# A hybrid diffusion layer on one core: the middle stage reordered

## The reference

```python
h = rmsnorm(x, norm1_g) * (1 + sc1) + sh1
z = h @ w_in                                  # 1280 columns
u_ssm, u_pool, u_conv = z[..., :512], z[..., 512:768], z[..., 768:]
# A) two-way diagonal complex scan (32 groups of 16 channels, 64 states), then
y = gelu(y); y_ssm = y * sigmoid(y @ w_glu + b_glu)
# B) pooling: mean over centred windows 2/4/8/16 minus the token, 64x64 linear per group, scale
# C) v = a * sigmoid(g); depthwise convolution of width 31; LayerNorm over 256 channels; silu
x = x + g1 * (concat(y_ssm, y_pool, y_conv) @ w_out)
h2 = rmsnorm(x, norm2_g) * (1 + sc2) + sh2
x = x + g2 * ((silu(h2 @ w1) * (h2 @ w3)) @ w2)
```

## Time and profile before

| | us |
|---|---|
| runs (median; lowest, highest) | 1330.0; 1328.51, 1331.0 |
| the profiled execution: span from the first to the last instruction | 1323.8 |
| PE busy (share of the span) | 1220.8 (92%) |
| DVE busy | 850.8 (64%) |
| ACT busy | 511.0 (39%) |
| POOL busy | 516.0 (39%) |

### The profile page before, as it was taken

How to read it: one execution, slowest core, us unless ns; L and a number is a source line. 1 busy time by engine, 2 the same in 40 slices (tenths; PEclk the granted TensorE clock), 3 DMA queues, 4 the chain that set the end, 5 groups by cost and what they waited for, 6 DMA issues and landing times.

```text
span 1323.8 us, 21436 instructions
## 1 busy us (share of the span) xinstructions
PE 1220.8 (92%) x7574; PEld 1080.5 (82%) x7574; DVE 850.8 (64%) x1338; ACT 511.0 (39%) x911; POOL 516.0 (39%) x360
## 2 busy tenths in 40 slices
PE   6786978995599999899999999999999999999996
PEld 4486877895545788799999999999889999999995
DVE  5538539959973427677666667766865555555558
ACT  2652531117235646633333333333532333334223
POOL 0595104376233101654444455444443233333340
PEclk9897988898799999999999999999999999999998
DMA  8815054389791331866665766666768777777771
GB/s 308 339 64 157 28 163 150 105 95 211 204 400 64 128 112 64 270 225 221 206 217 187 246 222 227 217 207 220 260 193 276 246 256 256 260 254 263 244 275 75
DMA packets 189570, 268.52 MB, mean 203 GB/s; under 512 B 14031, under 2 KB 108537, under 8 KB 186825
## 3 DMA queue, kind: packets, MB, share of 16 engines
q1 hardware_dynamic: 188144, 263.07, 60.6%
q0 software_dynamic: 1280, 4.72, 0.9%
q10 hardware_dynamic: 88, 0.02, 0.0%
HBM read 186.49 MB, written 81.26 MB: 202 GB/s over the span
## 4 chain that ended last, share of the span: by engine, by line
PE 76%; DMA 5%; issue 4%; POOL 4%; ACT 4%; DVE 3%; SPq 3%; DVEq 0%; ACTq 0%; POOLq 0%
PE banks L862 22%; PE banks L864 22%; PE banks L863 22%; PE banks L1131 3%; DMA ad<-in_ada_w 1%; PE banks L898 1%; PE banks L947 1%; SPq L436 1%; ACT nts L1660 1%; PE banks L1013 1%; POOL psum_w L751 1%; POOL sst L791 1%; DMA z_dram<-zp 1%; POOL pu L757 1%; PE banks L1136 1%
## 5 line engine op out<-in xcount | busy, mean ns | idle before, releaser
L814 POOL TENSOR_TENSOR raw13r<-raw13s,w13h 128x512 fp32r<-128x512 f32 x110 | 155.1, 1418 | 467.1 <-ACT w13h L1612 421.9
L863 PE MATMUL banks<-ntr,w13h 128*128 128x256 f32 (+1 forms) x1144 | 336.1, 294 | 0.0
L862 PE MATMUL banks<-ntr,w13h 128*128 128x256 f32 (+1 forms) x968 | 282.5, 292 | 4.4 <-ACT xs L1622 2.3
L863 PEld LDWEIGHTS banks<-ntr,w13h 128*128 128x128 f32 x1144 | 215.5, 188 | 0.9
L862 PEld LDWEIGHTS banks<-ntr,w13h 128*128 128x128 f32 x968 | 182.5, 189 | 6.5 <-ACT xs L1622 2.6
L862 PE MATMUL banks<-f2h,f_hi 128*128 128x512 f32 x396 | 156.6, 395 | 0.4 <-DVE acc L2317 0.4
L864 PE MATMUL banks<-f2h,f_lo 128*128 128x512 f32 x396 | 156.2, 395 | 0.0
L863 PE MATMUL banks<-f2l,f_hi 128*128 128x512 f32 x396 | 156.2, 394 | 0.0
L864 PE MATMUL banks<-ntr,raw13r 128*128 128x256 f32 (+1 forms) x528 | 153.5, 291 | 0.0
L2183 DVE TENSOR_TENSOR acc<-acc,banks 128x512 f32<-128x512 f32 x170 | 112.7, 684 | 38.9 <-PE banks L864 30.8
L818 POOL TENSOR_TENSOR f2l<-f2s,f2h 128x1024 fp32r<-128x1024 f32 x44 | 106.1, 2432 | 34.1 <-ACT f2h L1616 34.1
(11 more groups left out here) (323 smaller groups left out, 2536.4 us busy)
## 6 DMA issues: line engine op xcount, KB each, us to landing
raw13s<-in_ffn_w SPq DMA_DIRECT2D x66, 512.0 KB, 4.5
parts<-w13h SPq DMA_DIRECT2D x110, 256.0 KB, 2.4
w13h<-parts SPq DMA_DIRECT2D x110, 256.0 KB, 2.7
f2s<-in_ffn_w SPq DMA_DIRECT2D x44, 512.0 KB, 4.2
ad<-in_ada_w SPq DMA_DIRECT2D x20, 1024.0 KB, 9.8
parts<-wsumr SPq DMA_DIRECT2D x66, 256.0 KB, 2.6
wsumr<-parts SPq DMA_DIRECT2D x55, 256.0 KB, 4.9
parts<-raw13r SPq DMA_DIRECT2D x44, 256.0 KB, 2.9
```

The lines of the kernel that those rows point to most:

```text
L814: nc.gpsimd.tensor_tensor(w13_low(x, f), w13_low(x, f, F32), w13h[x][:, :, :].bitcast(F32), ALU.subtract).then_inc(sem("w13_lo"), 1)
L862: nc.tensor.matmul(out, hi_w, hi_x, start=start, stop=False)
L863: nc.tensor.matmul(out, hi_w, lo_x, start=False, stop=False)
```

## The change

It does seven things.

1. `sst` is split into four quarter buffers. Quarter 0 lies in the buffer of the pooling windows (`psum_w`), and is copied by POOL alone, all 8 copies, right after the pooling, ahead of the second gate of the convolution input and without waiting for the input projection's end. Of quarters 1 to 3 POOL copies the rows r = 0 and ACT the rows r = 1, in the order of the quarters. `yb` moves to where the copy of quarter 0 was.
2. The first gate of the convolution input goes ahead of the second half of the pooling's second part (`gate_conv(0)` after `w_low(9)`).
3. `u9` has four buffers. Re-reads 2 and 3 are issued after the `wc` reads of quarters 1 and 2, no longer in the transposes' loop.
4. Of quarter 3's eight writes of y four are issued by ACT.
5. PE runs GLU tile 2, the rest of adaLN group 2, and GLU tile 3 directly; the first channel means come behind them, then three of the blocks' first products, and only then the second channel means. ACT's squares and roots move behind `y_high(3)`, its SiLUs to the end of the stage.
6. `OUT` takes y parts 2 and 3 before the convolution's 6 and 7.
7. The low parts of y parts 0 to 3 go from DVE to POOL, one after each `wo_low`.

The diff, with the changed lines and some of those around them:

```diff
--- before.py
+++ after.py
@@ -200,14 +200,14 @@
-    u9 = [at(f"u9{i}", [P, 8, UC], O_UZ + 9216 + 4608 * i) for i in range(2)]
+    u9 = [at(f"u9{i}", [P, 8, UC], a) for i, a in enumerate((O_UZ + 9216, O_UZ + 13824, O_WS + 9216, O_WS + 13824))]
...
-    sst = at("sst", [P, 2, Q, UC], O_NT + 36864)
+    sst = [at(f"sst{e}", [P, 2, 2, 4, UC], O_WB + 9408 if e == 0 else O_NT + 36864 + 9216 * e) for e in range(4)]
...
-    yb = [at(f"yb{i}", [P, 8, UC], O_WB + 9408 + 4608 * i) for i in range(2)]
+    yb = [at(f"yb{i}", [P, 8, UC], O_NT + 36864 + 4608 * i) for i in range(2)]
@@ -217,7 +217,7 @@
-    OUT = (4, 5, 0, 1, 6, 7, 2, 3)
+    OUT = (4, 5, 0, 1, 2, 3, 6, 7)
@@ -347,6 +347,11 @@
     def low_ready(i):
...
+
+    def row_copy(e, r, d, par):
+
+        return (view(sst[e], (2 * par + d) * 4 * UC, [[UC, 4], [BL, NBL], [1, BL]], NS * r, NS),
+                view(st, r * Q * SLOTS + NPAIR * d + 4 * e, [[1, 4], [Q, NBL], [SLOT, BL]], NS * par, NS))
@@ -458,7 +463,7 @@
         def u_again(j):
...
-                sp.dma_start(u9[j % 2][16 * s:16 * s + 16, :, :],
+                sp.dma_start(u9[j][16 * s:16 * s + 16, :, :],
@@ -478,6 +483,8 @@
+            if e in (1, 2):
+                u_again(e + 1)
         def out_weights(n):
@@ -487,16 +494,15 @@
-            if j + 2 < 4:
-                sp.wait_ge(sem("y_done"), 2 * (j + 1))
-                u_again(j + 2)
-            for t in range(CH):
+            for t in range(CH if j < 3 else CH // 2):
...
-                sp.wait_ge(sem("st_copied_act"), 16)
-                sp.wait_ge(sem("st_copied_pool"), 16)
-            sp.wait_ge(sem("y_out"), 16 * 8 * (j + 1))
+                sp.wait_ge(sem("st_copied_act"), 12)
+                sp.wait_ge(sem("st_copied_pool"), 20)
+            if j == 3:
+                sp.wait_ge(sem("y_out_act"), 64)
+            sp.wait_ge(sem("y_out"), 16 * 8 * (j + 1) if j < 3 else 448)
@@ -527,7 +533,7 @@
-        sp.wait_ge(sem("y_low_dve"), 4)
+        sp.wait_ge(sem("y_part_pool"), 6)
...
         def w13_in(pr, f, tile, first=False):
@@ -734,6 +740,12 @@
+        def gate_conv(j):
+            pool.wait_ge(sem("z_evac"), NB * (8 + 2 * j))
+            for a0, b0, n in ((PAD, 0, LAT), (PAD + LAT + PAD, LAT, CTX)):
+                nc.gpsimd.tensor_tensor(vp[:, j, a0:a0 + n], vp[:, j, a0:a0 + n], sig[:, j, b0:b0 + n], ALU.mult).then_inc(sem("gated"), 1)
+            pool.wait_ge(sem("gated"), 2 * (j + 1))
+
@@ -757,12 +769,17 @@
+                    if j == 1:
+                        gate_conv(0)
...
-        for j in range(2):
-            pool.wait_ge(sem("z_evac"), NB * (8 + 2 * j))
-            for a0, b0, n in ((PAD, 0, LAT), (PAD + LAT + PAD, LAT, CTX)):
-                nc.gpsimd.tensor_tensor(vp[:, j, a0:a0 + n], vp[:, j, a0:a0 + n], sig[:, j, b0:b0 + n], ALU.mult).then_inc(sem("gated"), 1)
+        pool.wait_ge(sem("scan_done"), 1)
+        for r in range(2):
+            for d in range(2):
+                for par in range(2):
+                    nc.gpsimd.tensor_copy(*row_copy(0, r, d, par)).then_inc(sem("st_copied_pool"), 1)
+        pool.wait_ge(sem("st_copied_pool"), 8)
+        gate_conv(1)
         def wo_low(n):
@@ -776,20 +793,16 @@
-                pool.wait_ge(sem("y_low_dve"), m - 1)
+                pool.wait_ge(sem("y_part_pool"), m + 1)
...
-        pool.wait_ge(sem("gated"), 4)
...
-        pool.wait_ge(sem("scan_done"), 1)
-        for e in (0, 2):
-            for r in range(2):
-                for d in range(2):
-                    q0 = NPAIR * d + 4 * e
-                    for par in range(2):
-                        nc.gpsimd.tensor_copy(view(sst, (par * Q + q0) * UC, [[UC, 4], [BL, NBL], [1, BL]], NS * r, NS),
-                                              view(st, r * Q * SLOTS + q0, [[1, 4], [Q, NBL], [SLOT, BL]], NS * par, NS)).then_inc(sem("st_copied_pool"), 1)
+        for e in range(1, 4):
+            for d in range(2):
+                for par in range(2):
+                    nc.gpsimd.tensor_copy(*row_copy(e, 0, d, par)).then_inc(sem("st_copied_pool"), 1)
+        pool.wait_ge(sem("st_copied_pool"), 20)
@@ -797,6 +810,7 @@
+            y_low(m, ym[m % 2][:, :], m + 3)
@@ -1100,16 +1114,18 @@
-                pe.wait_ge(sem("st_copied_act" if j % 2 else "st_copied_pool"), 8 * (j // 2 + 1))
+                pe.wait_ge(sem("st_copied_pool"), 8 + 4 * j)
+                if j:
+                    pe.wait_ge(sem("st_copied_act"), 4 * j)
...
-                    mm(out, toep[:, 2 * gp + par, :], u9[j % 2][:, (2 * gp + par) % 8, :], start=True, stop=False)
-                    mm(out, wc[:, par, gp, HD:HD + P], sst[:, par, gp, :], start=False, stop=False)
-                    last = mm(out, wc[:, par, NPAIR + gp, 0:P], sst[:, par, NPAIR + gp, ::-1], start=False, stop=True)
+                    mm(out, toep[:, 2 * gp + par, :], u9[j][:, (2 * gp + par) % 8, :], start=True, stop=False)
+                    mm(out, wc[:, par, gp, HD:HD + P], sst[j][:, par, 0, gp % 4, :], start=False, stop=False)
+                    last = mm(out, wc[:, par, NPAIR + gp, 0:P], sst[j][:, par, 1, gp % 4, ::-1], start=False, stop=True)
@@ -1143,18 +1159,14 @@
+        glu_tile(2)
+        ada_tiles(2, 3, KT, B[4])
+        ada_bias_add(2, B[4])
+        glu_tile(3)
...
-        glu_tile(2)
-        for b in range(NB):
-            pe.wait_ge(sem("dev_squared"), 2 * (b + 1))
-            channel_mean([lnw[:, 0, :], lnw[:, 1, :]], b)
-        ada_tiles(2, 3, 6, B[4])
-        glu_tile(3)
-        ada_tiles(2, 6, KT, B[4])
-        ada_bias_add(2, B[4])
-        ready = {4: ("y_part_pool", 1), 5: ("y_part_pool", 2), 0: ("y_low_dve", 1), 1: ("y_low_dve", 2), 2: ("y_low_dve", 3), 3: ("y_low_dve", 4),
+        ready = {4: ("y_part_pool", 1), 5: ("y_part_pool", 2), 0: ("y_part_pool", 3), 1: ("y_part_pool", 4), 2: ("y_part_pool", 5), 3: ("y_part_pool", 6),
...
         def out_part(c, n0, n1, wait=False):
@@ -1175,14 +1187,17 @@
+        for b in range(NB):
+            pe.wait_ge(sem("dev_squared"), 2 * (b + 1))
+            channel_mean([lnw[:, 0, :], lnw[:, 1, :]], b)
...
+        for c in range(4):
+            out_part(c, 4, 6, c == 0)
...
-        for c in range(4):
-            out_part(c, 4, 6, c == 0)
@@ -1481,12 +1496,9 @@
         def state_copy(e):
-            for r in range(2):
-                for d in range(2):
-                    q0 = NPAIR * d + 4 * e
-                    for par in range(2):
-                        A_(view(sst, (par * Q + q0) * UC, [[UC, 4], [BL, NBL], [1, BL]], NS * r, NS),
-                           view(st, r * Q * SLOTS + q0, [[1, 4], [Q, NBL], [SLOT, BL]], NS * par, NS), ACT.Copy).then_inc(sem("st_copied_act"), 1)
+            for d in range(2):
+                for par in range(2):
+                    A_(*row_copy(e, 1, d, par), ACT.Copy).then_inc(sem("st_copied_act"), 1)
         def y_out(c):
@@ -1509,13 +1521,18 @@
+        state_copy(2)
+        y_out(2)
+        y_out(3)
...
-        for c in range(2, 6):
+        for c in range(4, 8):
...
+        act.wait_ge(sem("y_evac"), 16)
+        for t in range(CH // 2, CH):
+            act.dma_start(dview(y_dram, 3 * P * CH * UC + t * UC, [[CH * UC, 16], [16 * CH * UC, 8], [1, UC]]),
+                          yb[1][16 * t:16 * t + 16, :, :]).then_inc(sem("y_out_act"), 16)
...
-        y_out(6)
...
-        y_out(7)
@@ -1547,7 +1564,6 @@
-        act.wait_ge(sem("y_out"), 512)
@@ -1558,29 +1574,30 @@
+        glu_gate(2)
+        wo_high(4)
+        act.wait_ge(sem("scan_done"), 1)
+        mod_row_out(2, B[4])
+        act.wait_ge(sem("ada_tile"), 2 * KT + 4)
+        act.wait_ge(sem("glu_made"), 3)
+        y_high(2, ym[0][:, :])
+        glu_gate(3)
+        wo_high(5)
+        act.wait_ge(sem("glu_made"), 4)
+        y_high(3, ym[1][:, :])
...
-        glu_gate(2)
-        wo_high(4)
...
-        glu_gate(3)
-        act.wait_ge(sem("scan_done"), 1)
-        mod_row_out(2, B[4])
-        wo_high(5)
-        act.wait_ge(sem("ada_tile"), 2 * KT + 4)
-        conv_silu(0)
...
-        conv_silu(1)
-        for m in (2, 3):
-            act.wait_ge(sem("glu_made"), m + 1)
-            y_high(m, ym[m % 2][:, :])
...
+        conv_silu(0)
+        conv_silu(1)
@@ -2024,10 +2041,6 @@
-        def y_low(m):
-            dve.wait_ge(sem("y_part_act"), m + 3)
-            TT(y_lo[m][:, :], ym[m % 2][:, :], y_hi[m][:, :].bitcast(F32), ALU.subtract).then_inc(sem("y_low_dve"), 1)
-
@@ -2049,8 +2062,6 @@
-        y_low(0)
-        y_low(1)
@@ -2061,8 +2072,6 @@
-        y_low(2)
-        y_low(3)
...

```

## The result

The changed kernel takes 1336.71 us as the median of 10 runs (1332.80 to 1343.44), the kernel before 1328.03 (10 runs, 1322.40 to 1332.47): ratio 1.0068, 95% interval 1.0046 to 1.0090, so slower, by about 9 us. The profiled run of the changed kernel took 1342.24 us with a span of 1340.4.

The account below looks back on a forecast made before the run. The prediction took the chain of waits, mostly TensorE's products, to bound the kernel; -3.5 (transposes) + 2.4 (adaLN stall) + 5.4 (tail) + 2.0 (clock) = +6.3 on 1330.0 gave 1336.3 us, 8-in-10 range 1328 to 1342.

Parts of the forecast that it names:

- part (b): SyncE's y transposes, write, landing and read-back four times: GLU starts at 359.6 instead of 363.06, -3.5 us.
- the tail: Output products from the second channel means on: TensorE waits for y parts 6 and 7, +5.4 us (4.4 to 6.5).
- Part (a): Convolution gate and state-row copies on POOL: taps about 7.3 us earlier, first y product near 308, worth 0.
- take 8.3: Transposes, first to second read-back: 8.3 us instead of 12.6, as re-read 3 leaves this step.
- second to third stays 6.2: Transposes: the step from second to third read-back keeps its 6.2 us.
- 4.4: Transposes, third to fourth read-back: 4.4 us instead of 7.0, with GELUs done earlier and half the writes on ACT.
- The rule of ring order: DMA queue ahead of the y write: descriptors go in ring order, so re-read 3 delays the first read-back 3.5 us.
- rival 2: First y write passes the queue: first read-back at 327, GLU at 349.3, sum -4.0, 1326.0 us; chance 0.13.
- The adaLN stall: Last adaLN group after GLU tile 2: TensorE waits for tile 7's load, +2.4 us (1.0 to 4).
- table 1.28: ACT, after the scaling and before the SiLU pairs: a table load of 1.28 us on the way to y6.
- The clock: TensorE's granted clock falls after the tail's two gaps, +2.0 us (0 to 3); for the adaLN gap 0.
- Rival 3: Both gaps pull the clock down long and the last ada load meets other traffic: +12.4, 1342.4 us; chance 0.12.

Follow-up runs that it names:

- experiment 1: Changed kernel with the new order of TensorE's work, OUT and low parts undone; copies, buffers, re-reads and write split stay: 1328.05 us, ratio 1.0001 to before.
- experiment 7: Changed kernel with re-read 3 issued behind the first quarter's y writes instead of ahead of them: 1331.96 us (1 run).
- experiment 8: Changed kernel with GLU and output weights issued while SyncE waits for y writes to land, and adaLN biases put to the end: 1328.98 us (1 run).
- experiment 3: Changed kernel with adaLN tile 3 of group 2 made ahead of GLU tile 2 instead of behind it: 1333.3 us (1 run).
- experiment 9: kernel 4 with the first channel means between adaLN tiles 6 and 7 of group 2: 1325.23 us (1 run).
- experiment 2: Kernel before with only the new order of GLU, adaLN, means and y parts, and low parts on POOL: 1335.38 us, ratio 1.0058.
- kernel 4: Changed kernel with first means and squares ahead of GLU tile 3, second means right behind it, roots ahead of y_high(3): 1335.76 us (1 run).
- kernel 12: kernel 10 with re-read 3 behind the first y writes, ahead of the state-copy wait, and output weights behind the second and third quarters' writes: 1320.94 us, ratio 0.9928.
- kernel 5: Kernel before, with POOL waiting for VectorE's subtraction w_lo(1) before the third piece of wc: 1326.69 us, ratio 0.9997.
- experiment 6: Kernel before, with VectorE holding w_lo(1) until POOL has begun its wc products, so that both run together: 1329.82 us (1 run).
- kernel 10: Kernel of experiment 9 with the loads of experiment 8 and the wait of kernel 5: 1321.34 us, ratio 0.9943.

## Why the prediction was right, and where its sum was not

Forecast 1336.3, measured 1336.71. From R to c4 the sum gave +6.3, and the traces give 150.6 for 144.2, +6.4. But that exactness is luck: two errors cancel, part (b) 2.7 too good and the tail 2.5 too bad. That the times agree within 0.4 is luck too: the base of 1330.0 was 2.0 above the median of ten runs, and the change 2.4 more than forecast.

- **Part (a), 0.** Right in result: experiment 1 moves G by 0.4. The copies and taps moved as worked out (the taps end 77.0 after R for 84.5, so 7.5 earlier, forecast 7.3); TensorE reads them only at 420.00, so no one was waiting. The first y product, 8.1 after R, was expected 8.2 after it.
- **Part (b), -3.5: only -0.8.** The first read-back was right: +3.2 for +3.5, and experiment 7 shows that this is re-read 3's place ahead of the first write. The step that failed is the one where I took the time back, "take 8.3", "second to third stays 6.2", "4.4": measured 9.37, 7.45 and 5.04, 3.0 us more in all. I had the writes landing 2 us behind the last issue, and eight issues at 3.9. They landed 3.6, 2.3 and 2.8 behind it, and the issues took 4.43 and 4.78. The median from issue to landing went from 2.8 to 4.0; DMA issues of this stretch, first of the kernel before (300 to 365 us), then of the changed one (300 to 372):

```profile
y_dram<-yb SPq DMA_DIRECT2D x32, 72.0 KB, 2.8
```

```profile
y_dram<-yb SPq DMA_DIRECT2D x28, 72.0 KB, 4.0
```

What it is in the queue that makes them slower was not tried, so the cause stays open.

- **The rule of ring order.** It held: what is taken from ahead of the first write brings the first read-back forward (experiment 7: -3.3 without re-read 3; experiment 8: -4.2 without 1.0 MB of GLU weights and the adaLN biases). The Trainium skill (DMA: Bandwidth & Descriptors, Queues, rings and completion order) says that each DMA engine consumes its ring in order; these runs agree. By it rival 2 was out, and it was: the changed kernel has no read-back before 37.
- **The adaLN stall, +2.4.** Measured 2.28. Experiments 3 and 9 show that it was the load behind tile 3's slot: with tile 3 taken earlier, or with 4.2 us of mean products ahead of tile 7, the gap before tile 7 is gone. Experiment 3 also shows what I had left out: tile 3's own load is on the way until 27 us after G, so to take that tile earlier only moves the wait.
- **The tail, +5.4: +2.9** (88.1 - 80.9, less stall and clock). The kind was right (two waits at y parts 6 and 7, put down to DVE's low part), the size not. y6 and y7 were used 16.7 and 19.9 us after the second means' start, for 18.8 and 22.1. The term mis-sized is ACT's: I had put a table load of 1.28 into the way twice, as "table 1.28" ahead of the SiLUs and inside the 3.5 us from the second means to the reciprocals. Both loads ran while ACT was waiting, at 427.15 and 438.98, ahead of the root at 433.80 and the SiLU at 444.13. The reciprocals began 2.2 us after the means' start, not 3.5. In the kernel before, ACT came to the root's load only when its other work was done, and the root waited for it:

```profile
400.92 1.04 ACT L1481 CAST wo<-wos 128x1024 fp32r<-128x1024 f32 x1
401.97 1.28 ACT L1570 ACT_TABLE_LOAD   x1
403.27 1.76 ACT L1570 ACTIVATE lnr<-banks,eps 128x389 f32<-128x389 f32 x3
```

The Trainium skill (ScalarE: Activation LUTs, What ACT_TABLE_LOAD costs) gives about 1283 ns for such a load and about 1380 ns more of drain at each switch. The rows have 1.28 for the load, so its price was right and its place wrong; the drain doesn't show, for the load begins 0.01 after the cast ends and the root 0.02 after the load, and here the measurement decides.
- **The clock, +2.0.** Measured 2.0: the ten matmuls from 452.20 to 456.55 took 4.35 us, and would take 2.3 at the 0.23 from start to start that the later ones have. The size is luck in part: I had taken it for gaps of 3.8 and 2.6, and they were 1.9 and 2.1. Rival 3 (a long low clock and other traffic) didn't come. For the adaLN gap of 2.3 I took 0: the windows behind it show 1.00, and behind it the eight matmuls take 1.06 or 1.07 in four more traces (experiments 2, 4, 7 and 8, gaps of 2.37 to 2.46). But behind a gap of 2.03 at another tile experiment 3 shows 1.54, so the length of a gap alone doesn't decide, and the 0 was luck and not knowledge.
- **What the sum can't hold.** The two medians differ by 8.7, the marks by 6.4 up to c4. Behind c4, where the code is the same, the changed trace is 1.5 longer. There its granted clock is 0.98 where the trace before has 1.00 (100 to 200 us behind c4) and 0.99 (400 to 600 us behind it), while one wait for ACT (`xs`) is 1.1 shorter; what lowers the clock there was not tried. Other traces lie from -1.0 to +2.6 of before behind c4. Whether the rest of the 8.7 is upstream scatter is not shown.

## What to carry to other kernels

Before work is moved out from under another engine's cover, work out from the last row of that chain when its result is wanted; a reordering that takes no work from TensorE pays only by the waits, and the lower clock behind them, that it removes (kernel 4: the norm moved ahead, c4 5.1 us earlier after G). In this kernel loads were best put behind the write whose landing the issuing engine must wait for anyway: kernel 12 has 1.6 MB more there than the changed one, its first read-back is at 30.3 after R and not at 37.3, and its three steps from read-back to read-back sum to 21.9 as in that one, while 0.6 MB ahead of that write cost 3.2 us. When you work out such a chain from rows, count a table load of ACT only where ACT has no idle time ahead of it.

## What was not expected of the hardware

A DVE subtraction of two SBUF operands all but stands still beside POOL's products. In the changed kernel, DVE, then POOL:

```profile
65.34 8.74 DVE L1898 TENSOR_TENSOR w_lo<-wst,w_hi 128x1024 fp32r<-128x1024 f32 x1 [2.52 <-ACT w_hi L1363]
```

```profile
64.32 1.12 POOL L707 DMA_DIRECT2D wc_dram<-wct  x2 [0.30 <-POOL wct L704]
65.46 1.23 POOL L697 TENSOR_TENSOR wct<-powr,cc 128x576 f32<-128x576 f32 x1
...
73.29 1.12 POOL L707 DMA_DIRECT2D wc_dram<-wct  x2 [0.30 <-POOL wct L704]
```

In the kernel before, the same operation took 1.23 us, while POOL issued DMAs:

```profile
64.43 1.23 DVE L1881 TENSOR_TENSOR w_lo<-wst,w_hi 128x1024 fp32r<-128x1024 f32 x1 [2.52 <-ACT w_hi L1348]
```

In the changed kernel it began 0.1 us before six products of POOL and ended at 74.08, only after POOL had turned to its next issues; POOL's own products took 1.22 to 1.43, as before. Of the nine traces with neither the guard (kernel 5's wait) nor the forced collision three show this (8.74, 9.05, 9.03), and experiment 6 brought it about by a wait. The Trainium skill (GPSIMD Engine Reference, Specifications) says that the SBUF interfaces are shared, with contention where DVE has two SBUF inputs; the runs agree and add that this DVE operation can lose nearly everything until POOL pauses. DVE operations with one operand in PSUM keep their 0.68 to 0.69 us (128x512) beside the same products of POOL, in the kernel before from 101.64 on, as they do at 440.06 with POOL idle.

What it costs further on can be read from R. Among the nine traces and experiment 6, the six without the collision have R at 299.8 to 301.1, the four with it at 302.7 to 309.6 (experiment 6 at 304.0). POOL's first subtraction `w_lo` starts at 184.0 to 186.8 in the six and at 190.4 to 193.1 in the four. So some 4 to 6 us go with the collision by then. But kernels with the guard and without the collision start there at 185.0 to 189.8, so the 8.8 of the changed trace are not explained by the collision alone, and R differs by 11.6 us between kernels 10 and 12, which both have the guard. That other source of the wander was not found, and the guard did not move the median in experiment 5.
